# Attention probabilities of the next to last head: turned through DRAM and VectorE instead of TensorE

## The reference, cut to what matters

```
z = h @ w_in                                  # 2048 -> 6656 columns, h = modulated rms_norm(x)
mixer A, 8 heads (differential attention):    # p = softmax(s1) - lam * softmax(s2); o = p @ v
mixer B, 8 query heads, 2 key heads (grouped-query attention)
o = concat(rms_norm(oa) * silu(ga), ob * silu(gb))
y = rms_norm(x + gate * (o @ w_out))
```

## Time and profile before

| | |
|---|---|
| median of 3 runs (lowest, highest) | 1234.78 us (1233.56, 1235.91) |
| the profiled execution, its own time | 1234.45 us |
| its span, first to last instruction | 1232.7 us |
| TensorE busy | 1191.3 us, 97% |
| VectorE, ScalarE, GpSimd busy | 839.1, 586.6, 255.0 us |
| mean granted TensorE clock | 0.996 |
| iterations 6 to 11 (heads by blocks) | 68.2 to 68.6 us each |
| iteration 12 (next to last head) | 79.36 us |
| iteration 13 (last head) | 76.49 us |
| iteration 14 (no attention) | 55.48 us |

### The profile page before, as it was taken

The page is one execution under the profiler, slowest core; times in us unless marked ns, Lnnn a source line. Parts: engine busy times, 40 slices in busy tenths (PEclk is TensorE's granted clock), DMA queues, the critical chain, the costliest instruction groups (busy, mean ns, idle before and its releaser), DMA issues.

```text
span 1232.7 us, 16454 instructions
## 1 busy us (share of the span) xinstructions
PE 1191.3 (97%) x5915; PEld 959.6 (78%) x5915; DVE 839.1 (68%) x1266; ACT 586.6 (48%) x1240; POOL 255.0 (21%) x439
## 2 busy tenths in 40 slices
PE   5899999999999999999999999999998999999996
PEld 4455788788887888888888888888877878788885
DVE  4455487877778777767676676767666574779764
ACT  5522234646546464546456554645556555212223
POOL 1211032011030210222222223222232313210111
PEclk9999999999999999999999999999999999999999
DMA  9999242636446375462635435353632422856644
GB/s 351 370 376 372 86 112 91 192 94 191 139 123 182 93 207 135 114 169 70 173 108 145 143 103 158 101 158 99 165 112 89 132 67 64 314 172 228 188 141 176
DMA packets 169777, 200.47 MB, mean 163 GB/s; under 512 B 11760, under 2 KB 129168, under 8 KB 168928
## 3 DMA queue, kind: packets, MB, share of 16 engines
q1 hardware_dynamic: 155824, 153.65, 41.0%
q0 software_dynamic: 13424, 45.20, 11.4%
q10 hardware_dynamic: 448, 0.57, 0.1%
HBM read 166.20 MB, written 33.18 MB: 162 GB/s over the span
## 4 chain that ended last, share of the span: by engine, by line
PE 79%; DVE 7%; DMA 5%; ACT 3%; SPq 3%; issue 2%; POOL 1%; DVEq 0%; ACTq 0%; POOLq 0%
PE z_ps L792 21%; PE z_ps L794 21%; PE z_ps L793 21%; PE ring L976 3%; PE ring L883 2%; SPq L702 2%; PE ring L980 2%; PE ring L818 2%; DMA row_st<-o_spill 2%; PE ring L916 2%; PE ring L917 2%; ACT s_sb L1262 1%; DVE gate_acc L1835 1%; DMA ada_raw<-in_w_ada_dram 1%; DVE small L1662 1%
## 5 line engine op out<-in xcount | busy, mean ns | idle before, releaser
L792 PE MATMUL z_ps<-w_hi,xt_hi 128*128 128x512 f32 x1350 | 544.4, 403 | 3.6 <-issue 1.1
L794 PE MATMUL z_ps<-w_hi,xt_lo 128*128 128x512 f32 x1350 | 527.1, 390 | 0.0
L793 PE MATMUL z_ps<-w_lo,xt_hi 128*128 128x512 f32 x1350 | 526.9, 390 | 0.0
L1099 ACT ACTIVATE w_hi<-w_raw 128x512 fp32r<-128x512 f32 x270 | 169.2, 628 | 378.2 <-PE z_ps L794 256.7
L792 PEld LDWEIGHTS z_ps<-w_hi,xt_hi 128*128 128x128 f32 x1350 | 254.2, 188 | 73.9 <-issue 27.0
L794 PEld LDWEIGHTS z_ps<-w_hi,xt_lo 128*128 128x128 f32 x1350 | 253.7, 188 | 54.6
L1561 DVE TENSOR_TENSOR w_lo<-w_raw,w_hi 128x512 fp32r<-128x512 f32 x270 | 193.8, 720 | 150.5 <-ACT w_hi L1099 150.1
L793 PEld LDWEIGHTS z_ps<-w_lo,xt_hi 128*128 128x128 f32 x1350 | 254.6, 189 | 43.4
L2045 POOL TENSOR_TENSOR sg<-sg,zs 128x128 f32<-128x128 f32 (+1 forms) x60 | 44.0, 733 | 428.0 <-DVE sg L1631 428.0
L1662 DVE TENSOR_REDUCE small<-s_sb 128x2 f32<-128x1536 f32 (+1 forms) x60 | 87.8, 1464 | 45.7 <-ACT s_sb L1099 45.7
L1262 ACT ACTIVATE s_sb<-s_sb,small 128x768 f32<-128x768 f32 (+1 forms) x120 | 98.1, 821 | 9.8 <-DVE small L1662 9.7
(11 more groups left out here) (200 smaller groups left out, 1316.5 us busy)
## 6 DMA issues: line engine op xcount, KB each, us to landing
w_raw<-in_w_in_dram SPq DMA_DIRECT2D x188, 256.0 KB, 3.4
ada_raw<-in_w_ada_dram SPq DMA_DIRECT2D x64, 512.0 KB, 11.7
p_spill<-s_sb SPq DMA_DIRECT2D x56, 384.0 KB, 2.8
w_raw<-in_w_out_dram SPq DMA_DIRECT2D x64, 256.0 KB, 4.0
p_pair<-p_spill SPq DMA_DIRECT2D x64, 192.0 KB, 3.9
gate_raw<-in_w_ada_dram POOLq DMA_DIRECT2D x12, 1024.0 KB, 8.4
p_block<-p_spill SPq DMA_DIRECT2D x96, 96.0 KB, 2.5
w_raw<-in_w_in_dram POOLq DMA_DIRECT2D x20, 256.0 KB, 6.3
```

The costliest lines, as they stand in the source:

```text
L792: pe.matmul(out, hi_l, hi_r, start=start, stop=False)
L793: pe.matmul(out, hi_l, lo_r, start=False, stop=False)
L794: return pe.matmul(out, lo_l, hi_r, start=False, stop=stop)
L1099: return act.activation(out, in_, ACT.Copy, **kw)
```

## The change

Group 11 is turned by blocks too: the bound of `by_blocks` moves by one, so that in iteration 12 the 24 TensorE transposes of tiles 1 to 4 and their eight ScalarE copies go, and SP's `move_rows` and `move_blocks` and VectorE's `turn_blocks` come for four tiles. The turn of the three PSUM banks shifts with it, as T1 to T4 take none. The gate of the last head, in iteration 13, is made at steps 4 to 8 instead of 4, 5, 7, 9, 11. The new table `STEPS_PE` would be for a mixer A head other than the last that is turned by TensorE; there is none, and `LAST_STEPS` keeps its contents, since its entries 10 to 15 are set right after.

```diff
-LAST_STEPS = {
+STEPS_PE = {
     1: [("O", -1)], 2: [("QK", 0)], 4: [("S", 0)], 5: [("S", 1)], 6: [("T", 0)], 7: [("S", 2), ("V", 0)], 8: [("T", 1)],
-    9: [("S", 3), ("V", 1)],
+    9: [("S", 3), ("V", 1)], 10: [("T", 2)], 11: [("S", 4), ("V", 2)], 12: [("T", 3)], 13: [("V", 3)], 14: [("T", 4)],
+    15: [("V", 4)],
 }
+
+LAST_STEPS = dict(STEPS_PE)
 LAST_STEPS[10] = [("T", 2), ("S", 4)]
...
 def by_blocks(a, t):
 
-    return t > 0 and KV_IT < a < OUT_IT - 2
+    return t > 0 and KV_IT < a < OUT_IT - 1
...
-    for kind, t in (LAST_STEPS if it == OUT_IT else STEPS_D if group_kind(it - 1) == "D" else STEPS).get(s, []):
+    a = it - 1
+    d_steps = STEPS_D if by_blocks(a, 1) else STEPS_PE
+    for kind, t in (LAST_STEPS if it == OUT_IT else d_steps if group_kind(a) == "D" else STEPS).get(s, []):
...
-GATE_AT = {4: 0, 5: 1, 7: 2, 9: 3, 11: 4}
+def gate_at(it):
+
+    return {4: 0, 5: 1, 7: 2, 9: 3, 11: 4} if by_blocks(it - 1, 1) else {s: s - 4 for s in range(4, 4 + TILES)}
...
-                    if s in GATE_AT and group_kind(it - 1) != "KV":
-                        gate_inverse(it - 1, GATE_AT[s])
+                    if s in gate_at(it) and group_kind(it - 1) != "KV":
+                        gate_inverse(it - 1, gate_at(it)[s])
...
-                    if s in GATE_AT and group_kind(it - 1) != "KV":
-                        gate_mul(it - 1, GATE_AT[s])
+                    if s in gate_at(it) and group_kind(it - 1) != "KV":
+                        gate_mul(it - 1, gate_at(it)[s])
```

## The result

Measured beside each other, the kernel before took 1235.56 us (median of 5 runs) and the changed one 1238.94 (5 runs): ratio 1.0033, interval [1.0018, 1.0047]. It is slower, by 4.1 us as the ratio has it; the ratio is not that of the two medians, which are 3.4 us apart. The profiled execution has a span of 1236.9 us against 1232.7; of the 4.2 us between them, 1.96 are there before iteration 12 begins (902.34 against 900.38), where the two kernels do the same work, and are not the change's.

What follows compares the result with a forecast made beforehand. The prediction took a loop of row loads through ScalarE, VectorE and GpSimd to pace iteration 12, not TensorE. Its terms, -0.75 for ScalarE and +1.57 for banks, summed to +0.8 us: 1235.6 us, range 1229.5 to 1239.0.

Steps and rivals of the forecast that it cites:

- the loop: Iteration 12: row load, ScalarE, VectorE, GpSimd, next row load; a turn takes 10.74 or 11.64 us, setting the pace.
- Transposes, waits and low clock of step 8 (0): Iteration 12: 8.0 us of TensorE time go, costed at nothing since the loop covers them; one 4 us wait replaces two.
- VectorE (0): Iteration 12: four added `turn_blocks` of 0.967 us in even steps, off the loop, cost 0; +3.9 us if all fell on it.
- ScalarE (-0.75): Iteration 12: eight copies to `pt_f` go; only the last pair, ahead of GpSimd's square, is on the chain: -0.75 us.
- SP (0): 20 added DMAs and two waits delay weight loads queued behind; the tightest still lands about 2.5 us early: 0.
- Row loads (0, -4.0 to +3.0): Loop's row loads share transfers with the blocks' DMAs: 0 taken, -4.0 us if all shortest, +3.0 if all longest.
- Banks (+1.57): Iteration 13: QK's part 0 waits for VectorE's second subtraction; step 3 starts 0.4 + 1.17 = 1.57 us later.
- Gate (0): Last head, iteration 13: five reciprocals and ten products move to earlier steps, no DMA moves with them: 0.
- TensorE the bound: Rival: TensorE sets the end, so 8.0 us go, 1226.8 us; chance 0.06 in full, 0.10 in part (1231.6).
- The clock falls at the new wait: Rival: iteration 13 step 2, TensorE's 2.4 us wait brings the low clock, costing 1.7: 1237.3 us; chance 0.15.
- What was to show it: Listed trace signs: 24 fewer transposes, four more block transposes, iteration 12 within 2 us of 79.36, waits in step 8, V3 or V4, QK.

Runs made afterwards that it cites:

- t4_early_banks: Changed kernel with T4 of group 11 one step earlier (13 instead of 14) and O, that head's output transposes, in banks 1 and 2: 1236.42 us beside after_banks.
- the crossing: Kernels with O, group 11's output transposes, in banks 1 and 2 against 2 and 0, for several orders of tile 4; banks 2 and 0 lose 0.21% on average.
- blocks_only: Changed kernel with the last head's gate at its old steps, so group 11 by blocks alone: 1239.83 us, ratio 1.0028 to the kernel before.
- after_banks: Changed kernel with only O, group 11's output transposes, put back in banks 1 and 2: 1238.47 us, run beside t4_early_banks.
- before_banks: Kernel before with only O, group 11's output transposes, put in banks 2 and 0, no tile of that head by blocks: slower by 0.24%.
- t4_pe: Changed kernel with tile 4 of group 11 back on TensorE, which also returns O to banks 1 and 2: 1235.76 us, ratio 0.9994 to the kernel before.
- t4_pe_banks: t4_pe with O, group 11's output transposes, in banks 2 and 0; own ratio not in the text, every such bank move lost 0.18 to 0.24%.
- gate_only: Kernel before with only the last head's gate at steps 4 to 8, group 11 still turned on TensorE: 1236.19 us, ratio 1.0000.
- t4_early: Changed kernel with T4 of group 11 one step earlier, 13 in place of 14: 1238.78 us, ratio 1.0021 to the kernel before.
- v4_late: Changed kernel with V4 of group 11 after the last tile of z in step 15 of iteration 12: 1239.10 us, ratio 1.0022 to the kernel before.

## Why the prediction was wrong

The forecast was 1235.6 us, 0.8 above before and called no change; the time is 0.33%, 4.1 us, above before. The step that failed is VectorE's: "I take 0", because `turn_blocks` stands in even steps and "nothing behind them is nearer to the loop than `row_lo`". Something is: V4, whose output ScalarE copies before it comes to the last row of the iteration and to the weights of the next. The order of the fourth block on VectorE costs 1.7 us where the sum has 0. The rest of the miss is ScalarE's 0.75 us, which did not show in the time, and some 1.0 us more at the banks than the 1.57 forecast, of which the clock is a likely but not a shown cause.

- **Transposes, waits and low clock of step 8 (0).** Right. One wait of 4.62 us on ScalarE's `o_sum` took the place of the two ("about 4"), and the clock was at 0.50 for 6.83 us, from 942.63, still in the wait, to 949.46. Steps 8 to 14 lose nothing that the loop doesn't cover: t4_early_banks keeps this wait and takes as long as before.
- **VectorE (0).** Wrong for the fourth block: 1.7 us by the crossing. Each transpose costs what the earlier trace rows say, 0.966 us against 0.967. But the fourth is not paid as VectorE's time. It stands behind the loop's row, ScalarE's copy before did not stand behind VectorE, and without T4 TensorE comes to V4 sooner, by the 0.69 us of six transposes. V4 waits 2.84 to 3.97 us in the changed order (after, blocks_only, after_banks) and 0.85 to 2.09 where ScalarE copies (before_banks, t4_pe, t4_pe_banks, gate_only; in the profiled execution of before there is no such wait, step 15 takes 4.76). The prediction named V4's wait and gave it no price. In the changed kernel's trace about 1.0 us of the 1.7 can be followed, through ScalarE's queue; in blocks_only's the loop is again the later of the two. How the 1.7 us divide over unprofiled runs was not tried.
- **ScalarE (-0.75).** In the traces it is there: the square that GpSimd needs for row 12 starts 1.16 us after the copy of row 10 (977.25 to 978.41) and before 1.91 (973.52 to 975.43). In the time it is not seen. t4_early_banks holds it, with all else of the blocks, at 1.0001 [0.9992, 1.0010]; a gain of 0.06% is within that.
- **SP (0).** No weight load was seen late. But the reads of the blocks are slower beside the row loads (median 4.1 us in iteration 12, 2.5 over the run): in t4_early VectorE's fourth transpose waits 0.41 us for `p_block`. In the changed kernel it does not, as the rows of `p_block` above show (977.4 against 978.02, where VectorE starts on the row ahead of it).
- **Row loads (0, -4.0 to +3.0).** The 14 legs together take 55.9, 60.2 and 56.3 us where no tile of that head goes by blocks (before, gate_only, before_banks) and 61.2 to 63.9 in the nine other executions that keep the loop's order. So they did lengthen, as the sentence of the Trainium skill ("DMA: Bandwidth & Descriptors", section "Issuing engines are not separate DMA queues") led one to expect. It didn't decide: in t4_early_banks the sum is 63.3 and the time that of before.
- **Banks (+1.57).** The mechanism was right, and in the traces nearly the size: 1.38 us. Of its two terms the 1.17 us measured 1.16 (994.93 to 996.09) and the 0.4 us 0.29 (1.03 from the pair's start to QK now, 0.74 before). By the ratios it is 2.6. A likely part of the rest is the clock behind the longer wait, 1.6 us more in v4_late and t4_early, none in five others with O in banks 2 and 0; as a mean over these seven executions that would be an estimate of 1.38 + 2/7 x 1.6 = 1.8 us, about as low as the four intervals allow. How often it falls in unprofiled runs stays open.
- **Gate (0).** Right: 1.0000.
- **The rivals.** "TensorE the bound" was not so in this kernel, but its number for iteration 12 was right: 71.4 us, and 70.96 once the loop is out of the way. "The clock falls at the new wait", given 0.15, had the right mechanism: the place was V4 in the changed kernel's profile and QK in two of the variants. The Trainium skill's sentence on it ("TensorE: Matmul & The Clock Gate", section "HAM oscillation — how this bites in real kernels") is that a long wait between groups of matmuls puts the array back on the low clock. The trace agrees at V4, where 2.84, 3.97 and 3.43 us of waiting were each followed by 0.50, and at S3. At QK the traces go both ways: 2.54 us in t4_early with a fall, 2.55 in before_banks without.
- **What was to show it.** Block transposes rose by four and iteration 12 shows 25 fewer records of TensorE, as said. It was to stay within 2 us of 79.36 and took 83.07, of which the spread of single executions (82.04 in gate_only) is a part. Step 8, V4's wait and QK's wait for `xt_lo` came as listed, and in iteration 13 the clock stayed at 1.00. The chain of waits of the changed kernel has no piece in iteration 12, so its round can't be read there; ScalarE's idle time before rows, 27.4 us, and the runs with the loop left out or put first say that the loop still paces it.

The sum as measured: 2.6 us for the banks and 1.7 for V4, 4.3 against 4.1 by the ratio.

## What to carry to other kernels

Work that a loop covers is free only as long as nothing it delays feeds that loop: follow the consumer of the moved work (here V4, the copy of its output, and what stands behind that copy in ScalarE's queue) to the path before writing 0. Removing an operation also moves every bank handed out behind it; print the banks before and after, and when an experiment puts an operation back, look whether it puts the banks back too. The gain was to be had elsewhere: the row load issued first in GpSimd's step gives 0.7% alone, and 1.0% with the blocks and the banks put right.

## What was not expected of the hardware

A wait of TensorE of 2.5 us at the same place was followed by the low clock in one kernel's execution and not in another's (2.54 and 2.55 us, above), so its cost can't be read off one profile. Two more go the same ways: 2.47 us in v4_late with a fall, 2.51 in t4_pe_banks without. The two with a fall also waited longer at V4 ahead of it (1.59 and 1.99 us against 0.85 and 1.38); whether that decides it was not tried. The low clock behind a wait took 1.3 us more for one tile of V (2.90 against 1.57) and lasted 3.4 or 6.8 us in the rows.
